# Queries of the first 256 tokens made inside the expert stage of a one-layer decoder step

## The reference, cut to what matters

```python
def peer(xn, w_pq, sub_keys1, sub_keys2, expert_u, expert_v):
    q = (xt @ w_pq).astype(jnp.float32).reshape(N, P_HEADS, 2, P_HALF)   # 8 heads x 2 halves x 128
    s1 = jnp.einsum('nhd,kd->nhk', q[:, :, 0], sub_keys1)                # 128 keys per half
    s2 = jnp.einsum('nhd,kd->nhk', q[:, :, 1], sub_keys2)
    v1, i1 = lax.top_k(s1, P_TOPK)                                       # 16 of 128, both halves
    v2, i2 = lax.top_k(s2, P_TOPK)
    ...                                                                  # 256 sums, the best 16
    idx = jnp.take_along_axis(cand_idx, top_p, axis=-1)
    g = jax.nn.softmax(top_s, axis=-1)
    ...
        u = expert_u[ids]
        a = jax.nn.gelu(jnp.einsum('pd,phkd->phk', xs, u), approximate=False)
        return jnp.einsum('phk,phkd->pd', (gs * a).astype(dt), expert_v[ids])
```

## Time and profile before

| | |
|---|---|
| median of 3 runs | 2473.68 us (2470.71 to 2474.11) |
| profiled execution | 2471.53 us, span 2469.7 us |
| mean granted clock of PE | 0.84 of full speed |
| busy: PE, DVE, ACT, POOL | 1855.8, 1509.9, 970.8, 666.3 us |
| HBM read, written | 711.16 MB, 16.66 MB |
| bytes of the gathers | 604.02 MB, queue q0 |

### The profile page before, as it was taken

The page is one execution under the profiler, slowest core; times in us unless marked ns, Lnnn a source line. Parts: engine busy times, 40 slices in busy tenths (PEclk is TensorE's granted clock), DMA queues, the critical chain, the costliest instruction groups (busy, mean ns, idle before and its releaser), DMA issues.

```text
span 2469.7 us, 29247 instructions
## 1 busy us (share of the span) xinstructions
PE 1855.8 (75%) x10168; PEld 1025.8 (42%) x10168; DVE 1509.9 (61%) x3441; ACT 970.8 (39%) x2481; POOL 666.3 (27%) x608
## 2 busy tenths in 40 slices
PE   7997699988869778776777676767666666666665
PEld 5775498756669674433333233322111111111110
DVE  3116534148745457776877776667666676666764
ACT  3223022321134446554444644444534343434343
POOL 0005000000000004443334344434444334434442
PEclk9998798989979899899989898888667676766676
DMA  4212332124164359999999999999999999999996
GB/s 156 76 43 72 110 108 63 37 69 136 64 227 167 121 187 373 417 417 409 416 418 417 411 417 418 414 415 416 420 421 417 420 419 410 421 418 417 417 415 272
DMA packets 163190, 732.55 MB, mean 297 GB/s; under 512 B 15217, under 2 KB 46005, under 8 KB 89192
## 3 DMA queue, kind: packets, MB, share of 16 engines
q0 software_dynamic: 82944, 604.02, 59.2%
q1 hardware_dynamic: 80104, 126.75, 15.5%
HBM read 711.16 MB, written 16.66 MB: 295 GB/s over the span
## 4 chain that ended last, share of the span: by engine, by line
DMA 45%; PE 8%; DVE 5%; ACT 4%; issue 2%; POOL 0%; ACTq 0%; POOLq 0%; DVEq 0%
DMA lower<-in_experts,upper 45%; PE bank L2203 5%; DVE lower L2052 4%; PE bank L1783 2%; ACT upper L2131 1%; ACT upper L2127 1%; ACT upper L2124 1%; ACT L2124 1%; ACT L2110 0%; PE bank L2177 0%; POOL lower L1980 0%; DVE upper_w_split L1681 0%; ACT upper_w_split L1620 0%; DVE lower L1697 0%; DVE upper L1691 0%
## 5 line engine op out<-in xcount | busy, mean ns | idle before, releaser
L2203 PE MATMUL bank<-lower,upper 64*64 64x512 f32 x4608 | 808.0, 792 | 459.8 <-ACT upper L2131 458.7
L1980 POOL DMA_INDIRECT lower<-in_experts,upper x576 | 629.5, 1093 | 1568.1 <-PE bank L2203 853.4
L2052 DVE SCALAR_TENSOR_TENSOR lower<-lower 128x1024 f32<-128x1024 f32 x576 | 705.5, 1225 | 447.1 <-DMA lower<-in_experts,upper 446.1
L2203 PEld LDWEIGHTS bank<-lower,upper 64*64 64x64 f32 x4608 | 147.6, 158 | 1023.8 <-ACT upper L2131 982.3
L2124 ACT ACTIVATE upper<-upper 128x1 f32<-128x1 f32 x576 | 116.4, 202 | 731.4 <-DVE lower L2052 730.2
L1783 PE MATMUL bank<-upper_x_split,upper_w_split 128*128 128x256 f32 (+1 forms) x2304 | 366.4, 318 | 43.4 <-DVE upper_w_split L1681 36.0
L1783 PEld LDWEIGHTS bank<-upper_x_split,upper_w_split 128*128 128x128 f32 x2304 | 338.9, 206 | 134.2 <-issue 82.4
L266 PE MATMUL bank<-upper_w_split,upper_x_split 128*128 128x512 f32 (+1 forms) x1200 | 277.6, 394 | 6.7 <-DVE upper_w_split L248 6.7
L266 PEld LDWEIGHTS bank<-upper_w_split,upper_x_split 128*128 128x128 f32 (+1 forms) x1200 | 214.8, 179 | 68.3 <-DVE upper_w_split L248 7.4
L2131 ACT ACTIVATE upper<-lower,upper 128x64 f32<-128x64 f32 x576 | 200.3, 348 | 19.1
L2127 ACT ACTIVATE upper<-upper 128x1 f32<-128x1 f32 x576 | 169.8, 295 | 53.8 <-ACT upper L2124 0.7
(11 more groups left out here) (249 smaller groups left out, 1630.7 us busy)
## 6 DMA issues: line engine op xcount, KB each, us to landing
upper<-in_w_in SPq DMA_DIRECT2D x40, 512.0 KB, 3.6
lower<-in_w_in SPq DMA_DIRECT2D x24, 512.0 KB, 3.6
lower<-in_experts,upper POOLq DMA_INDIRECT x576, 16.2
upper<-in_state_C SPq DMA_DIRECT2D x8, 1024.0 KB, 7.9
out_C_s<-upper SPq DMA_DIRECT2D x16, 512.0 KB, 3.5
upper<-in_w_pq SPq DMA_DIRECT2D x16, 512.0 KB, 3.6
upper<-in_w_in SPq DMA_DIRECT2D x32, 256.0 KB, 7.3
upper<-in_w_pq SPq DMA_DIRECT2D x32, 256.0 KB, 7.3
```

Source lines behind the costliest of these rows:

```text
L1980: pool.indirect_dma_start(ring[n % R], None, I["experts"], bass.IndirectOffsetOnAxis(numbers[:, g, k:k + 1], 0)).then_inc(arrived[n % R], 16)
L2052: dve.scalar_tensor_tensor(out=u, in0=u, scalar=1.0, in1=xn2[:, tile_of(g), :], op0=ALU.mult, op1=ALU.mult, accum_out=dots[:, g % 2, k:k + ...
L2203: ins = pe.matmul(sums_of(c)[i][j * QUAD:(j + 1) * QUAD, :], diag[half, n % NDIAG, :], ring[n % R][half, D + j * GRP:D + (j + 1) * GRP], s ...
```

## The change

What it does:

- `merge_first` makes no queries. Its merge has 10 groups and ends with the norm and the turned tokens `xn2T`, which stay in SBUF for the next stage.
- The merge of `experts` gets a lead of L = 4 query groups for FIRST (operand `xn2T`, 256 columns), ahead of its 14 groups: 18 groups, UNITS = 152. Group 0 makes heads 0 and 1 of both tiles, group 1 heads 2 and 3.
- Order at the start. PE: 8 units, the scores of rounds 0 and 1, 8 units, the scores of rounds 2 and 3, then the slots. DVE: 8 units, top16(0), 8 units, top16(1), then the dots. The other six pairs of rounds of FIRST are scored before slots 24, 40, 44, 48, 52 and 56 (`SCORE_AT`), in banks 6 and 7.
- `due`: HEAD = 16, BULK = 128 at slot 200, UNITS over 82 more slots; the merge ends at the same slot 282.
- The ring has 6 places for the gathers of slots 0 to 47 (GROW = 48) and 8 after; the two others lie on `xnT`, and slot 54 waits until group 4, which reads it, is split.
- The lead queries lie in `branch[1]`, `junk` and `g_row` in place of `qpT`, so the row of norm weights is loaded only when all scores of FIRST are made.

The diff, cut to its core:

```diff
@@ merge_first and its caller @@
-        qpT = A.take(2 * PH, FIRST_TOK, at=at_yrT)
-            env["junk"] = A.take(D, at=at_kT)
-            env["xn2T"] = A.take(KD, FIRST_TOK, at=at_kT + D)
+            env["xn2T"] = A.take(KD, FIRST_TOK, at=at_kT)
+            env["junk"] = A.take(D, at=at_kT + KD * FIRST_TOK)
-            units = Pace(merge.scalar(act))
-            units.until(merge.BRANCHES * merge.U)
-            act.wait_ge(moved, 64)
-            units.all()
+            Pace(merge.scalar(act)).all()
@@ Merge @@
+        self.lead, self.lead_query, self.lead_free = lead if lead else (None, None, None)
+        QG = 2 * PH // self.NB4
+        self.L = QG if lead else 0
+        self.GATES, self.BRANCHES, self.QUERIES = (self.L + self.XG * i for i in (2, 4, 5))
+        self.NG = self.QUERIES + (QG if query else 0)
+    def columns(self, g):
+        return FIRST_TOK if g < self.L else self.n
-                if u == 1 and 1 <= g <= self.GATES:
+                if u == 1 and self.L < g <= self.GATES:
+                    if self.L and g == self.L + self.XG + 1:
+                        act.wait_ge(*self.lead_free)
                     gates(g - 1)
-                if u == 1 and g > self.QUERIES:
+                if u == 1 and (g > self.QUERIES or 2 < g <= self.L):
                     keep_queries(g - 1)
+                if u == U - 1 and g < min(self.L, 2):
+                    keep_queries(g)
@@ experts @@
-    HEAD, BULK_SLOTS, BULK, REST_SLOTS = 8, 190, 96, 92
+    HEAD, BULK_SLOTS, BULK, REST_SLOTS = 16, 200, 128, 82
+    R0, GROW = R - 2, 8 * (R - 2)
+    def place(n):
+        return n % R0 if n < GROW else (n - GROW) % R
+    def before(n):
+        if n < GROW:
+            return n - R0 if n >= R0 else None
+        if n - GROW < R:
+            return GROW - R0 + place(n) if place(n) < R0 else None
+        return n - R
+    SCORE_AT = {24: 2, 40: 3, 44: 4, 48: 5, 52: 6, 56: 7}
-                if g == 0:
+                if g == merge.L + merge.XG:
+                    sp.wait_ge(scored, NROUND // 2)
                     sp.dma_start(g_row, I["norm2_row"].broadcast_to([P, D])).then_inc(merge.row, 16)
-                if n == 4:
-                    pool.wait_ge(scored, NROUND // 2)
-                if n == 6:
-                    pool.wait_ge(merge.lo, merge.U)
-                if n >= R:
-                    pool.wait_ge(used, n - R + 1)
+                if n == GROW + R0:
+                    pool.wait_ge(merge.lo, merge.U * (merge.L + 1))
+                if before(n) is not None:
+                    pool.wait_ge(used, before(n) + 1)
             units = Pace(merge.vector(dve))
+            units.until(HEAD // 2)
             for part in range(LINKS + 1):
                 top16(0, part)
             weights_of(0)
-            units.until(HEAD // 2)
+            units.until(HEAD)
             for part in range(LINKS + 1):
                 top16(1, part)
             units = Pace(merge.scalar(act))
-            for i in range(NROUND // 2):
-                keep_scores(i)
-            units.until(2)
+            units.until(HEAD // 2)
+            keep_scores(0)
+            units.until(HEAD // 2 + 2)
             exps(0)
+            units.until(HEAD)
+            keep_scores(1)
             units.until(HEAD + 1)
-            for i in range(NROUND // 2):
-                if i >= 4:
-                    pe.wait_ge(kept_scores, i - 3)
+            for i in range(2):
+                units.until(HEAD // 2 * (i + 1))
+                pe.wait_ge(merge.kept, merge.NB4 * (i + 1))
                 score(i)
-            pe.wait_ge(kept_scores, NROUND // 2)
-            units.until(HEAD)
+                if n in SCORE_AT:
+                    i = SCORE_AT[n]
+                    pe.wait_ge(kept_scores, i - 1)
+                    pe.wait_ge(merge.kept, merge.NB4 * min(i + 1, merge.L))
+                    score(i)
```

More of the change, by code:

```diff
@@ L1565, in __init__ @@
         w_pq = blocks_of(I["w_pq"])
-        self.weights = [whole[g // self.XG][:, :, (g % self.XG) * GRP:(g % self.XG + 1) * GRP] for g in range(self.QUERIES)]
-        self.weights += [w_pq[:, :, j * GRP:(j + 1) * GRP] for j in range(self.NG - self.QUERIES)]
+        queries = [w_pq[:, :, j * GRP:(j + 1) * GRP] for j in range(QG)]
+        self.weights = queries[0:self.L]
+        self.weights += [whole[g // self.XG][:, :, (g % self.XG) * GRP:(g % self.XG + 1) * GRP] for g in range(5 * self.XG)]
+        self.weights += queries[0:self.NG - self.QUERIES]
         self.arrived = [sem(f"{name}_w_arrived{i}") for i in range(self.NF)]
@@ L1588, in operand @@
     def operand(self, g):
-        if g in (0, self.GATES, self.GATES + self.XG):
-            return self.operands[(0, self.GATES, self.GATES + self.XG).index(g)]
+        if g == 0 and self.L:
+            return self.lead
+        if g in (self.L, self.GATES, self.GATES + self.XG):
+            return self.operands[(self.L, self.GATES, self.GATES + self.XG).index(g)]
         if g == self.BRANCHES:
@@ L1646, in keep_queries @@
                 act.wait_ge(self.steps, self.product_done(g, j))
-                act.activation(self.query((g - self.QUERIES) * NB4 + j), self.bank(g, j)[:, 0:self.n], ACT.Copy).then_inc(self.kept, 1)
-        for g in range(self.NG):
+                dst = self.lead_query(g * NB4 + j) if g < self.L else self.query((g - self.QUERIES) * NB4 + j)
+                act.activation(dst, self.bank(g, j)[:, 0:self.columns(g)], ACT.Copy).then_inc(self.kept, 1)
+        for g in range(self.NG + 1):
             if g == self.BRANCHES:
@@ L1824, in merge_first @@
     merge = Merge(env, "p5", FIRST, 2, [bank[0:4], bank[4:8]], [bank[2:4], bank[6:8]], xnT[:, :, first], yrT[:, :, first],
-                  hmT[:, :, first], branch, lambda b: qpT[:, b, :], x1, xn2, g_row)
+                  hmT[:, :, first], branch, x1, xn2, g_row)
     moved = sem("p5_moved")
@@ L1897, in query, with lead_query @@
         return branch[1][:, b, :] if b < PH else branch[0][:, b - PH, :]
+    spare = [branch[1].rearrange("p k t -> p (k t)"), junk, g_row]
+    def lead_query(b):
+        per = [t.shape[1] // FIRST_TOK for t in spare]
+        for t, n in zip(spare, per):
+            if b < n:
+                return t[:, b * FIRST_TOK:(b + 1) * FIRST_TOK]
+            b -= n
+    scored = sem("p6_scored")
     merge = Merge(env, "p6m", LAST, 1, [bank[2:6]], [bank[2:4], bank[4:6]], env["xnT"][:, :, FIRST_TOK:], yr_last, hm_last,
-                  branch, query, x1, xn2, g_row)
+                  branch, x1, xn2, g_row, lead=(lead_x, lead_query, (scored, NROUND // 2)), query=query)
     UNITS = merge.NG * merge.U + 1 + merge.norm_steps + 1
@@ L2049, in dot @@
                 g, k = n // TOPK, n % TOPK
[L2050 to L2051 removed]
+                u = ring[place(n)][:, 0:D]
+                dve.wait_ge(arrived[place(n)], 16 * (turn_of(n) + 1))
                 dve.scalar_tensor_tensor(out=u, in0=u, scalar=1.0, in1=xn2[:, tile_of(g), :], op0=ALU.mult,
@@ L2193, in _ @@
                     pe.wait_ge(kept_scores, i - 1)
-                    pe.wait_ge(merge.kept, merge.NB4 * min(i - NROUND // 2 + 1, PH // 2))
+                    pe.wait_ge(merge.kept, merge.NB4 * (merge.L + min(i - NROUND // 2 + 1, PH // 2)))
                     score(i)
+                if n in SCORE_AT:
[3 more added lines that the diff above has]
+                    score(i)
+                if first and c == 1:
+                    pe.wait_ge(kept_scores, NROUND // 2)
                 if first and c >= 2:
@@ L2203, in _ @@
                         ins = pe.matmul(sums_of(c)[i][j * QUAD:(j + 1) * QUAD, :], diag[half, n % NDIAG, :],
-                                        ring[n % R][half, D + j * GRP:D + (j + 1) * GRP], start=first, stop=last)
+                                        ring[place(n)][half, D + j * GRP:D + (j + 1) * GRP], start=first, stop=last)
                 ins.then_inc(used, 1)
```

59 lines of the change are left out of this document (36 added, 23 removed).

## The result

The changed kernel takes 2465.62 us in the median of 7 runs (2461.63 to 2468.13), the kernel before 2474.04 (2470.37 to 2474.97). The ratio is 0.9968 with a 95% interval of 0.9958 to 0.9978: 8 us faster, 0.3%, forecast at 6.7 us (2467.0). The profiled execution of the changed kernel took 2467.62, its span is 2465.8.

A forecast was written before the change was run, and what follows sets the result against it. Bound by the gathers' DMA bytes in the experts stage; -24.1 + 15.1 + 1.3 + 1.0 = -6.7 us takes the profiled 2471.53 to 2464.8, for the median 2467.0, range 2459 to 2475.

The forecast's parts named there:

- Steps 1 to 3: Start of last stage: first load at 841.2, first lead group kept at 863.2, first gather at 874.0, 32 us earlier.
- Step 4: Second lead group: weight loads queue behind gathers, unit 15 comes at 893.9, first dot at 904.1, 28.7 us earlier.
- the 908: Start of the slots: a first dot after 908 us would make the forecast wrong.
- Step 5: Seventh gather: waits for a freed place 4.9 us after the first dot, goes at 909.0; DMA resumes 24.1 us earlier.
- Step 6: Bytes left at the seventh gather: 15.1 us more for unit loads, 1.3 for norm weights, 1.0 for the thinner refill queue.
- Step 7: The slots: extra scores and 0.56 units per slot in place of 0.46 cost nothing, covered by idle PE and DVE.
- Rate: Full DMA part: 417 GB/s as traced; at the skill's 358 the extra bytes cost 19.0 us, not 16.4, sum -4.1.
- One: Gathers 6 to 53: six places don't keep DMA full if landings stay 16.2 us; 25 us lost, 2492; chance 0.08.
- Two: Start of last stage: lead groups take longer, first dot about 907.7, sum -3.1, 2470.6 us; chance 0.14.
- three: The slots: no longer bound by DMA, 17 us of the 24 units' product exposed, 2484 us; chance 0.04.
- four: Lead groups: loads don't bind in the second and PE sets the first; -16.6 us at most, about 2461; chance 0.10.
- step 2: First lead group: first load lands at 844.8, PE begins at 846.9, eight units take 15.6 us, last block kept at 863.2.

The follow-up runs named there:

- gathers_later: The changed kernel with POOL holding the first gather until DVE has split unit 11 of the lead groups: 2460.86 us, ratio 0.9951 to the kernel before.
- half_weights: The changed kernel with the last stage's merge weight loads fetching only half the columns from the third group on: 2428.81 us, ratio 0.9813 to the kernel before.
- ring6_all: The changed kernel with a ring of 6 places for all 576 slots, not only the first 48: 2472.08 us, ratio 0.9992 to the kernel before.
- ring4_all: The changed kernel with a ring of only 4 places for all slots: 2721.01 us, ratio 1.099 to the kernel before.

## Why the prediction was right

**Steps 1 to 3.** First gather forecast at 874.0 - 841.0 = +33.0, measured +33.3. The first load took 3.2 us (847.21 to 850.45), the eight units, their keeping and all up to the first score 16.7 from the first product (852.50 to 869.17) where I had 16.3.

**Step 4.** First dot forecast at +63.1, measured +60.9. The weights behind the gathers did bind, as the row of before had said, with waits of 1.9, 3.3 and 2.5 us, but for three units only; I had all four 3.1 us apart after a wait of 8.7. `gathers_later` shows that the gathers caused these waits: it took them out of the way of the loads, and the seventh gather came 4.8 us earlier. The first dot at 907.63 kept just under the 908 that I had named as a sign of being wrong, but only because the 5.7 us by which the norm ended later are in it; counted from the norm's end there was room.

**Step 5.** From the first dot to the seventh gather 4.6 us, forecast 4.9. Together with step 4 the resumption came 26.7 us earlier relative to the norm's end, forecast 24.1. This is the only term of the sum off by more than a us, 2.2 of it from step 4, and it is what makes -9.6 in the profiles of -6.7.

**Step 6.** From the seventh gather to the end: 2465.8 - 912.2 = 1553.6, before 2469.7 - 933.14 = 1536.6; 17.0 more, forecast 15.1 + 1.3 + 1.0 = 17.4. No run separates its three terms; the 1.0 for the refill was a guess. The price of a load, 0.63 us, is borne out by `half_weights` within its interval.

**Step 7.** Nothing, as put: with half of the loads' bytes PE and DVE went faster through the same work.

**Rate.** 412 to 418 GB/s in the full part, in windows of 125 us and more (before, the slices have 409 to 421, where I had read 410). The Trainium skill's 358 ("DMA: Bandwidth & Descriptors", Specifications) would have made 19.0 of step 6's 16.4. It is given there as half of what two cores share; here one core runs, and the trace stands above it to the end.

**Rivals.** One (a landing keeps its length) is refuted by 11.3 and 7.9 us, and in the changed kernel itself by 13.3 in slots 8 to 45. That is more than the 12 that I forecast and the 13.0 that I allowed, and DMA was full all the same: these gathers go out 2.8 us apart, so a place waits 6 x 2.8 - 13.3 = 3.5 us after a landing, not 4.2. The part of the rival that is true is that eight places are worth 6.5 us later on, which the change keeps. Two (lead groups slower) and three (slots bound by engines) didn't come. Of four, 2.2 of the 5.9 us of step 4 came, and nothing of the 4 of step 2.

**The part before the norm's end** took 5.7 us longer in one profile than in the other. At 570 us the changed kernel is 2.1 us behind, which I didn't take apart. Of the other 3.6 at least a part is PE's clock: the same 8 matmuls take 1.06 us in the profile of before, at 2.4 GHz, and 1.88 in the other, most of it at the lower level of 1.2; the mean granted clock of the 20 us around them is 0.91 and 0.83. Before each group PE had idled for the same 0.67 us.

```profile
604.55 1.06 PE L1417 MATMUL bank<-lower 128*128 128x128 f32 x8 [0.67 <-DVE upper L1283]
600.00:620.00 20.00, 16.66 (x72) 10.55 (x72) 17.10 (x35) 1.49 (x5) 0.00 (x0) 0.91 0.64 211
```
```profile
606.63 1.88 PE L1416 MATMUL bank<-lower 128*128 128x128 f32 x8 [0.67 <-DVE upper L1282]
600.00:620.00 20.00, 17.42 (x69) 11.95 (x68) 18.42 (x39) 1.49 (x5) 0.00 (x0) 0.83 0.66 210
```

Why the clock was granted otherwise in two executions of the same instructions stays open. `ring6_all`, with the change, has 1.07 us and 0.91 and ends the norm at 840.96, so the change alone doesn't do it. Seen from the span alone the profiles differ by 3.9 us, with these 5.7 taken out by 9.6; the medians, at 8.4, lie between.

## What to carry to other kernels

Where DMA is full to the end and its rate stays the same, count how many bytes it has moved by the point from which it stays full; neither the first transfer nor the first consumer tells the time. Starting the bulk early pays only as far as it doesn't stand ahead of the small loads that the next step waits for: here holding the first gathers back by 9 us, until the last weights had been asked for, cost nothing and probably gained 3 to 5. A ring may be short in a stretch where little work lies between landing and release, and its size there is tested by bandwidth, not by the landing time, which is mostly the queue.

## What the runs showed of the hardware that was not expected

The part before the norm's end, the same instructions in all kernels with the change, ended between 840.96 (`ring6_all`) and 847.37 us (`ring4_all`) in the profiles, which is most of what the change itself gains; runs of the changed kernel spread as much (2461.63 to 2468.13). Part of it is the clock granted to PE between 600 us and the norm's end, as shown above. And the busy share of the DMA engines is a poor measure of their rate: 1.02 went with 415 GB/s, 0.97 with 372.
